# Latent attention two heads at a time: value products in 64-column groups, and the sums of the weights on GpSimd

## What is computed

```python
def dense_attention(q, k, v, scale):
    ...
        s = jnp.einsum('bqhgd,bkhd->bhgqk', qb, k).astype(jnp.float32) * scale
        p = jax.nn.softmax(s, axis=-1).astype(v.dtype)
        return jnp.einsum('bhgqk,bkhv->bqhgv', p, v)

def prefix_attention(q, k, v, q_c, k_c, v_c, scale, need_ctx):
    o = dense_attention(q, jnp.concatenate([k, k_c], axis=1), jnp.concatenate([v, v_c], axis=1), scale)
    o_c = dense_attention(q_c, k_c, v_c, scale) if need_ctx else None
    return o, o_c

def mla_mixer(h, h_c, rows, need_ctx, w_in, g_qa, w_qb, g_kva, w_kvb):
    ...
        q = (rms_norm(q_lat, g_qa) @ w_qb).reshape(bsz, n, A_HEADS, A_NOPE + A_ROPE)
        kv = (rms_norm(kv_lat, g_kva) @ w_kvb).reshape(bsz, n, A_HEADS, A_NOPE + A_V)
    ...
    o, o_c = prefix_attention(q, k, v, q_c, k_c, v_c, (A_NOPE + A_ROPE) ** -0.5, need_ctx)
    return gated(o, gate), (gated(o_c, gate_c) if need_ctx else None)
```

## Time and profile before

| | us |
|---|---|
| median of 3 runs | 1667.3 (1667.1 to 1669.59) |
| span of the profiled execution | 1666.1 |
| PE busy | 1582.5 (95%) |
| DVE busy | 1006.0 (60%) |
| POOL busy | 915.0 (55%) |
| ACT busy | 696.4 (42%) |
| latent attention, from the first scores to the last values | 859.3 to 1121.8 |

### The profile page before, as it was taken

How to read it: one execution, slowest core, us unless ns; L and a number is a source line. 1 busy time by engine, 2 the same in 40 slices (tenths; PEclk the granted TensorE clock), 3 DMA queues, 4 the chain that set the end, 5 groups by cost and what they waited for, 6 DMA issues and landing times.

```text
span 1666.1 us, 28604 instructions
## 1 busy us (share of the span) xinstructions
PE 1582.5 (95%) x11752; PEld 1282.3 (77%) x11752; DVE 1006.0 (60%) x1308; ACT 696.4 (42%) x1210; POOL 915.0 (55%) x722
## 2 busy tenths in 40 slices
PE   6999888999999999999989999999989999999887
PEld 5677787678888888878877777768877888888775
DVE  5699785746565540052465756664766665656566
ACT  4653775333222220042336565661154344444562
POOL 5354787838999999964550321346524444444152
PEclk9999999999999999999999999999899999999998
DMA  5221104422322243341120000003321101111211
GB/s 194 76 90 62 54 4 156 152 102 76 101 101 87 89 159 119 116 150 51 51 76 1 26 1 26 1 4 148 127 90 51 48 29 51 51 51 51 102 51 51
DMA packets 18881, 126.15 MB, mean 76 GB/s; under 512 B 2096, under 2 KB 2352, under 8 KB 4304
## 3 DMA queue, kind: packets, MB, share of 16 engines
q1 hardware_dynamic: 18624, 124.02, 21.2%
q10 hardware_dynamic: 144, 0.52, 0.1%
HBM read 122.43 MB, written 2.10 MB: 75 GB/s over the span
## 4 chain that ended last, share of the span: by engine, by line
PE 54%; issue 19%; POOL 12%; DVE 9%; ACT 4%; DMA 1%; POOLq 0%; ACTq 0%; SPq 0%; DVEq 0%
POOL w_hi L672 8%; PE banks L1324 5%; PE banks L1303 4%; POOL w_lo L663 4%; PE banks L1481 4%; PE banks L1484 4%; PE banks L1482 4%; PE banks L1186 3%; PE banks L1191 3%; PE banks L1187 3%; PE banks L1536 2%; PE banks L781 2%; PE banks L782 2%; PE banks L783 2%; PE banks L1516 2%
## 5 line engine op out<-in xcount | busy, mean ns | idle before, releaser
L672 POOL TENSOR_TENSOR w_hi<-raw,der 128x512 fp32r<-128x512 f32 x296 | 333.8, 1138 | 419.8 <-PE banks L1484 186.9
L663 POOL TENSOR_TENSOR w_lo<-raw,w_hi 128x512 fp32r<-128x512 f32 x336 | 479.6, 1440 | 61.9 <-ACT w_hi L1624 61.6
L781 PE MATMUL banks<-h_hi,w_hi 128*128 128x512 f32 x464 | 184.2, 397 | 0.3 <-DVEq L2308 0.3
L782 PE MATMUL banks<-h_lo,w_hi 128*128 128x512 f32 x464 | 180.7, 389 | 0.0
L783 PE MATMUL banks<-h_hi,w_lo 128*128 128x512 f32 x464 | 180.6, 389 | 0.0
L1481 PE MATMUL banks<-h_hi,w_hi 128*128 128x512 f32 (+1 forms) x384 | 146.3, 381 | 0.1
L1482 PE MATMUL banks<-h_lo,w_hi 128*128 128x512 f32 (+1 forms) x384 | 131.0, 356 | 0.0
L2145 ACT ACTIVATE dP<-banks,der 128x768 f32<-128x768 f32 x64 | 57.8, 902 | 160.2 <-DVE der L2981 160.2
L725 POOL TENSOR_TENSOR Of<-Of,Ls 128x768 f32<-128x768 f32 x8 | 14.7, 1834 | 186.6 <-DVE Ls L2783 186.6
L1484 PE MATMUL banks<-h_hi,w_lo 128*128 128x512 f32 (+1 forms) x384 | 116.1, 356 | 0.0
L781 PEld LDWEIGHTS banks<-h_hi,w_hi 128*128 128x128 f32 x464 | 87.1, 188 | 25.9 <-issue 7.5
(11 more groups left out here) (514 smaller groups left out, 3856.9 us busy)
## 6 DMA issues: line engine op xcount, KB each, us to landing
raw<-in_stream SPq DMA_DIRECT2D x84, 1024.0 KB, 4.9
ada_raw<-in_ada_w SPq DMA_DIRECT2D x18, 1024.0 KB, 7.1
raw<-in_ada_w SPq DMA_DIRECT2D x4, 1024.0 KB, 4.8
xT<-in_x_t SPq DMA_DIRECT2D x2, 1024.0 KB, 6.6
xT<-in_x_t SPq DMA_DIRECT2D x1, 2048.0 KB, 7.9
ada_end<-in_ada_w SPq DMA_DIRECT2D x2, 1024.0 KB, 5.9
out_t<-z SPq DMA_DIRECT2D x8, 256.0 KB, 2.1
ctxT<-in_ctx_t SPq DMA_DIRECT2D x1, 1024.0 KB, 6.9
```

The costliest lines, as they stand in the source:

```text
L663: return pool.tensor_tensor(lo[:, h, part(i), :], raw_tiles(half)[:, part(i), :], hi[:, h, part(i), :], ALU.subtract)
L672: pool.tensor_tensor(hi[:, h, part(i), :], raw_tiles(half)[:, part(i), :], one, ALU.mult).then_inc(hi_done, 1)
L781: pe.matmul(banks[b][:, :], hi, tile(rhs_hi, k), start=(at_k == 0), stop=False)
L782: pe.matmul(banks[b][:, :], hi, tile(rhs_lo, k), start=False, stop=False)
```

## The change

- PE computes the value products of both heads of a pair in one step: two fp32 products with 64 columns of weights each, one into the upper and one into the lower 64 partitions of bank 2. The steps of the two heads alternate (s = 0 to 13, head e = s % 2), the values follow in the odd s.
- The value tile has no ones and is one tile for the pair. The sums of the weights are made apart: POOL adds the exponentials of the pair's six key tiles (`add_part`, five additions of 128x1024 to Sx and one of 128x512 to Sc), and PE multiplies the sum with 64 columns of ones (`sums_x`, `sums_c`) in the next pair's steps 2 and 8, into bank 3. In the last pair DVE does these additions (`last_part`).
- ACT copies the result once for a pair (512 columns and 256) and no sums; DVE inverts straight out of PSUM. `finish` is cut in a part of 512 columns and one of 256.
- POOL's splits are cut in pieces between the additions.
- Queries have four buffers, exponentials three of 2x512, Of and Ls one. The order of every engine is written anew, the start of the stage too: `tops` of heads 0 and 1 go between the last input projections.

The core of the difference (buffer addresses, the sums behind the stage and the waits for counts that follow from the pairs are left out):

```diff
-        def values(h, j):
+        def values(p, j):
...
             if j < 6:
-                mm = pe.matmul(pairs[1][:, 0, :], v[:, j, :], Pf[:, i % 4, :], start=(j == 0), stop=(j == 5), skip_group_check=True)
+                for e in range(2):
+                    mm = pe.matmul(banks[2][HEAD[e], :], v[:, j, HEAD[e]], weighed[:, e, :], start=(j == 0), stop=(j == 5), skip_group_check=True)
...
+        def sums_x(p):
+
+            pe.wait_ge(*added(p, 5))
+            if p:
+                pe.wait_ge(sums_inverse, 3 * p)
+            for e in range(2):
+                mm = pe.matmul(banks[sum_bank(p, 0)][HEAD[e], :], ones[:, HEAD[e]], Sx[:, e, :], start=True, stop=True, skip_group_check=True)
+            mm.then_inc(sums_full.sem, 1)
...
+        scores(0)
+        for k in range(2):
+            query(2, k)
+        row(1)
+
+        TOP_SLOTS = [1, 2, 3, 4, 5, 7, 8, 9, 10, 11]
+        for p in range(N_PAIRS):
+            more = p < LAST_PAIR
+            for s in range(N_STEP):
+                if s == 6 and more:
+                    row(2 * p + 2)
+                if s == 12 and more:
+                    row(2 * p + 3)
+                if N_STEP * p + s + 1 < N_STEP * N_PAIRS:
+                    scores(N_STEP * p + s + 1)
+                if s == 0 and p == 0:
+                    key(1)
+                if more and s in (1, 2):
+                    query(2 * p + 3, s - 1)
+                if more and s in TOP_SLOTS:
+                    t = TOP_SLOTS.index(s)
+                    tops(2 * p + 2 + t // 5, t % 5)
+                if s == 2 and p:
+                    sums_x(p - 1)
+                if s == 8 and p:
+                    sums_c(p - 1)
+                if more and s in (5, 6):
+                    value_tokens(p + 1, range(3 * (s - 5), 3 * (s - 5) + 3))
+                if s in (8, 9) and p + 2 < N_PAIRS:
+                    query(2 * p + 4, s - 8)
+                if s == 12 and p + 2 < N_PAIRS:
+                    key(p + 2)
+                if s % 2:
+                    values(p, s // 2)
...
+            for s in range(N_STEP):
+                weigh_keys(N_STEP * p + s)
+                if s == 0 and p:
+                    output_c(p - 1)
...
+                if s == 0 and more:
+                    key_hi(p + 1, 1)
...
+                if s == 12:
+                    output_x(p)
+                if s == 13 and further:
+                    query_hi(2 * p + 4)
+                    key_hi(p + 2, 0)
...
+            top(a, 0)
+            top(a, 1)
+            rope_query(b)
+            rope_query_sum(b)
+            top(a, 2)
+            if p:
+                inverse(p - 1, 0)
+            top(a, 3)
+            top(a, 4)
```

More of the change, by code:

```diff
@@ L720, in _ @@
         assert (before - first) % 2 == 0
[L722 to L734 removed]
+        split(BLK1, 0, BLK1 // 2)
@@ new lines, in finish, with split_steps @@
+        def finish(p, c):
+            cols = slice(T, TA) if c else slice(0, T)
+            pool.wait_ge(sums_inverse, 3 * p + 2 + c)
+            pool.wait_ge(oc_copied if c else ox_copied, p + 1)
+            pool.tensor_tensor(Of[:, cols], Of[:, cols], Ls[:, cols], ALU.mult).then_inc(pair_divided, 1)
+            pool.wait_ge(pair_divided, 2 * p + 1 + c)
+            pool.tensor_tensor(gate_s[:, p, cols], gate_s[:, p, cols], Of[:, cols], ALU.mult).then_inc(pair_out, 1)
+        def split_steps(n, first, count):
+            split(n, half_of(n), n // 2, steps=range(first, first + count))
@@ new lines, in _ @@
+        n = BLK1 + 1
+        for p in range(LAST_PAIR):
+            first_half = p % 2 == 0
+            split_steps(n, 0 if first_half else 6, 2)
+            if not first_half:
+                n += 1
+            for j in (1, 2, 3):
+                add_part(p, j)
+                if first_half and j < 3:
+                    split_steps(n, j + 1, 1)
+            if p:
+                finish(p - 1, 0)
+            add_part(p, 4)
+            if p:
+                finish(p - 1, 1)
+            add_part(p, 5)
+            if first_half:
+                split_steps(n, 4, 1)
+            add_part(p, 6)
+            if first_half:
+                split_steps(n, 5, 1 if p < LAST_PAIR - 1 else 3)
@@ L735, in _ @@
+        n += 1
+        finish(LAST_PAIR - 1, 0)
+        finish(LAST_PAIR - 1, 1)
+        split_steps(n, 0, 2 * PARTS)
+        n += 1
+        finish(LAST_PAIR, 0)
+        finish(LAST_PAIR, 1)
         if n % 2:
@@ L1351, in _ @@
         key(0)
-        mla_in(10, range(0, 4))
-        value_tokens(0, range(6))
-        mla_in(10, range(4, KT))
-        for k in range(2):
-            query(1, k)
+        for k in range(KT):
+            mla_in(10, [k])
+            if k == 1:
+                for q in range(2):
+                    query(1, q)
+            if k == 4:
+                value_tokens(0, range(6))
+            if k >= 4:
+                tops(0, k - 4)
         for k in range(KT):
             mla_in(11, [k])
-            if k in (0, 2, 3, 5, 6):
-                tops(0, (0, 2, 3, 5, 6).index(k))
@@ L1361, in _ @@
-        row(0)
-        scores(0, 0)
-        for h in range(A_HEADS):
-            nxt, after = h + 1, h + 2
-            for j in range(N_S):
-                if j == 5 and nxt < A_HEADS:
-                    row(nxt)
-                if j < 6:
-                    scores(h, j + 1)
-                elif nxt < A_HEADS:
-                    scores(nxt, 0)
-                if j < 5 and nxt < A_HEADS:
-                    tops(nxt, j)
-                if after < A_HEADS:
-                    if j in (0, 2):
-                        query(after, j // 2)
-                    if h % 2 == 0 and j == 4:
-                        key(after // 2)
-                    if h % 2 and j in (4, 5):
-                        value_tokens(after // 2, range(3 * (j - 4), 3 * (j - 4) + 3))
-                values(h, j)
@@ L1382, in _ @@
-        pe.wait_ge(exp_done, N_S * A_HEADS)
+            if k == 0:
+                tops(0, 4)
+            if k == 2:
+                row(0)
+            if k >= 3:
+                tops(1, k - 3)
+        scores(0)
[31 more added lines that the diff above has]
+                    values(p, s // 2)
```

389 lines of the change are left out of this document (208 added, 181 removed).

## The result

| | before | after |
|---|---|---|
| median, us | 1667.3 | 1724.0 (1721.4 to 1725.2) |
| ratio after / before | | 1.0337, interval 1.0324 to 1.0350 |
| span of the profiled execution | 1666.1 | 1719.6 |
| end of the first `key_lo` of the loop | 880.2 | 871.5 |
| end of the seventh | 1081.0 | 1115.6 |

What follows compares the result with a forecast made beforehand. PE was taken to bound the kernel, busy 232.8 of 234.2 us in mid-stage. Three stretches, -5.8 (start), +26.2 (pairs 0 to 5) and +13.4 (end), sum to +33.8, taken as +33 on 1667.3: 1700 us, range 1676 to 1716.

Steps and rivals of the forecast that it cites:

- pair 0: First pair of the loop, without sums and inverses: 29.5 us of work, waits 1.7 + 1.6 + 2.3, half clock 1.5; put at 37.
- What PE is spared: PE's value products: 1.18 us a step side by side, saving 1.85 a pair; PE's work falls from 33.3 to 31.4.
- Rival (B): Values steps: the two column groups don't overlap, 1.72 us a step, total 1715; chance 0.10 together with rival (D).
- The four waits: New PE waits in each pair from the new order: 7.0 us summed, less 0.4, so 6.6; a pair takes 38.0.
- (1): First head, tops 1 to tops 4: DVE needs 6.8 us, PE 5.2, so PE waits 1.6; POOL adds 0.35 a pair.
- (2): Second head, tops 2 to tops 4: DVE needs 5.2 us, PE 4.0, so PE waits 1.2.
- (3): The second row, behind the query's sum and a reduction: 0.1 us of waiting without POOL, 1.45 more with POOL's addition.
- (4): The pair's boundary, from second row to next query: ACT and DVE need 7.3 us, PE 5.0, so PE waits 2.3.
- rival (D): Idle of 2.3 us at each pair's boundary lowers the clock, up to 1.7 a drop; chance 0.10 together with Rival (B).
- The start: To the end of the loop's first `key_lo`, at 874.5: 43.3 us, 5.8 less than before, with two casts at 3.08.
- The end: From the seventh `key_lo` to the last pair's product: 70 us instead of 56.8, put at 13.4 more.
- no meeting of POOL and DVE: Same waits in a pair, but POOL's additions miss DVE's sums: 36.6 us a pair; as rival 1690 to 1675, chance 0.12.

Runs made afterwards that it cites:

- Run 14: Run 12 with one POOL instruction moved: the low half of a split stands behind the third addition, not the second; 1667.4 us, ratio 1.000 to the kernel before.
- Run 1: The change with spare PE products of 512 columns put into its waits, adding nothing to the result: 1711.5 us, ratio 1.026 to the kernel before.
- run 8: Run 5 with start order and last OT_HI copy moved, value products one after the other over all 128 columns: 1707.4 us, against 1676.5 side by side.
- run 10: Run 5 with start order and last OT_HI copy moved, then DVE's query sum and last inverse, ACT's copies and POOL's context finish reordered: 1702.9 us, ratio 1.020.
- run 12: Run 11 with ACT's two late query copies moved and POOL's splits at the stage's end begun earlier: 1682.2 us, ratio 1.009 to the kernel before.
- run 5: The change with DVE's inverses and query sum moved, and the key ahead of the second row at the pair's boundary: 1679.8 us, ratio 1.007.
- run 11: Run 10 with the stage's end reordered, ACT's query copies moved (high half behind step 5's exponential) and fifth tops issued later: 1672.7 us, ratio 1.003.

## Why the prediction was wrong

By its own three stretches and the time behind them, in the profiled execution (1719.6, forecast 1699.1):

| | forecast | measured |
|---|---|---|
| first `key_lo` ends | 874.5 | 871.5, -3.0 |
| pair 0 | 37 | 37.3, +0.3 |
| pairs 1 to 5 | 190 | 206.8, +16.8 |
| to the last pair's product | 70 | 78.0, +8.0 |
| behind it | 528.3 | 526.0, -2.3 |

The rest, 0.7, is that 33.8 was rounded to 33. Two of the rows hold scatter. The count begins where the input projection of the last gates begins, and that was at 830.16 in this execution, 1.0 us before the 831.15 of the forecast; the 2.3 behind the last pair's product lie in the scatter of the part behind the output projection.

**What PE is spared: right.** A values step costs 1.20: from 1000.85 (the tops ahead of it start their last product of 0.12 at 1000.73) to 1002.28, less 0.23 for the first product of the next scores, where 1.18 was forecast from the 32-column pair of the earlier trace rows. Rival (B), no overlap, fell.

For the rest of the pair the waits have to be counted by the distance of starts, since the brackets count from the modelled end of a product. Take the first wait: the last product ahead of it starts at 1002.51, the second behind it at 1004.23. Between them lie two products of 0.23, so 1.26 us were lost, and not 0.99. Part of that is that a product which starts behind a wait, or behind another tiling, takes 0.34 and not 0.23 (1003.89 to 1004.23, and 1001.94 to 1002.28). Counted so, the five waits cost 1.26, 1.44, 1.41, 1.35 and 2.03, together 7.5, where the brackets say 6.36. PE's own work in a pair is then 38.7 - 7.5 = 31.2, as forecast (31.4). The pair of before holds 0.35 of waiting by the same count, so its work was 33.1, and 1.9 are saved, where 1.85 was forecast. Run 14's two waits cost 0.76 and 0.88 by this count, so it saves 33.1 - (33.2 - 1.6) = 1.5.

**The four waits: right in place, 0.9 short in size.** By the distance of starts: (1) 1.26 + 1.44 = 2.7, forecast 1.6 and 0.35 for POOL; (2) 1.4, forecast 1.2; (3) 1.35, forecast 1.55; (4) 2.0, forecast 2.3. Together 7.5, where the prediction summed to 7.0 and took 0.4 off, because a late reduction in (1) would partly hide in the next; (1) came out longer even without that. That an addition holds DVE's sum was right (2.04 where 2.1 was worked out); in (1) it does so in every pair and not in every other, and makes it 1.65 instead of 0.68. This misses the time by 0.7 us a pair, 3.5 us in pairs 1 to 5.

**The clock: the step that failed.** The prediction took one fall, at the start, into the sum, and as rival (D) wrote "A drop costs up to 1.7; included above 1700". The mechanism was named, and nothing was put into the sum for any later pair. The price was low too: no row shows 1.7, and the fall in the earlier trace rows cost 2.6 by the prediction's own count. The earlier trace rows had the warning: PE came back at half its clock from 3.97 us of idle, and the new order has idle of 1 to 2 us, four times in each of seven pairs, where before PE had 0.6% of idle in the whole loop. Measured: 13.3 us in pairs 1 to 5; in the rest of the stage (pair 6 from 1127.5 and the last pair from 1168.5) some 5 more, half of 6.8 and 3.4 us. A stretch of 6.8 us made a pair 2.7 to 3.2 us longer, two of 3.4 us together 2.8. Run 1 shows it as a cause, by 13.1 us in the same pairs. With hindsight the right term is one fall in most pairs; by an estimate of 2 to 3 us in six pairs from these figures the forecast would have stood at 1712 to 1718, and its range, moved as far, would have held the result. What sets off a fall in one pair and not in the next stays open.

**The start: 3 us better, 1 of them scatter.** The other 2 are the casts. The two casts of KLO took 1.11 us in all, not 3.08 as in the earlier trace rows. The trace of before has the reason, a POOL instruction that I had not laid beside them, and the change runs POOL's splits earlier:

```profile
861.53 3.55 POOL L663 TENSOR_TENSOR w_lo<-raw,w_hi 128x512 fp32r<-128x512 f32 x2
```

In the change:

```profile
867.45 1.11 DVE L2912 CAST KLO<-KLO 32x768 fp32r<-32x768 f32 x2
...
871.66 0.76 PE L1253 MATMUL banks<-lat_hi,w_hi 128*128 128x512 f32 x1 [6.64 <-DVE KLO L2857]
```

**The end: 8 us worse.** 4.4 of them lie in pair 6 (3.4 by the clock, an estimate: half of 6.8). In the last pair PE waited 2.78 us for an exponential behind a copy that waited for POOL's `finish`, where I had allowed 2.5 for all waits, and 0.78 again; then for low halves and the last chain:

```profile
1167.83 0.84 ACT L2120 ACTIVATE OT_HI<-gate_s 128x768 fp32r<-128x768 f32 x1 [3.38 <-POOL gate_s L769]
...
1169.21 1.98 PE L1390 MATMUL banks<-Pf,V 128*64 128x512 f32 x4 [2.78 <-ACT Pf L2104]
...
1181.67 0.50 PE L1253 MATMUL banks<-OT_HI,w_hi 128*128 128x512 f32 x1 [0.72 <-DVE OT_LO L2893]
...
1193.60 0.50 PE L1253 MATMUL banks<-OT_HI,w_hi 128*128 128x512 f32 x1 [1.59 <-DVE OT_LO L2893]
```

The two heads' products share their rows and differ in columns, and run side by side: the four records of a step span 1.08 us (the row at 1000.93), where the two of one head's full-width product span 1.02. A step costs 1.20, and run 8 pays 0.57 more. The rule of the Trainium skill that was weighed (TensorE: Matmul & The Clock Gate, Part 3: a weight load overlaps running products only where the row group differs) would have given 1.72 if taken at its word; here too the measurement decides against it.

**Three sums of the prediction don't come out as they are put.** With no meeting of POOL and DVE its own terms give 38.0 - 1.45 - 0.35 = 36.2 a pair and not 36.6; the last stretch, 70 less 56.8, is 13.2 and not 13.4; and the terms of pair 0 add to 36.6, put at 37. Each moves the time by less than 3 us, and none changes the outcome. Of the 3.0 us under the forecast at the start 1.0, and the 2.3 behind the stage, are scatter and not foresight; without them the miss in the profiled execution would be 23.8 and not 20.5, as it is 24 by the medians.

## What to carry to other kernels

Where a change gives a saturated TensorE idle of a microsecond or more, count the clock with it in every round of the loop: here the waits cost 7.5 us a pair, and the half clock, which came once or twice in four pairs of five, up to 4.7 more. A saving on the bounding engine is only as large as the slack of the chains that feed it; of 1.9 us a pair the best order tried kept 0.2 (33.23 against 33.46), and nothing of it shows in the time of the whole. And when an instruction is moved on one engine, look up who waits for it on every other: two of the orders tried here (runs 10 and 12) lost 26 and 10 us to a wait that the move itself had made.

## What the runs showed of the hardware

- The same waits did not always bring the half clock: of five pairs with the same waits one had none and another had it for some 10 us. In runs 5, 14 and 11, whose waits in pairs 1 to 5 are at most 0.5, 0.6 and 0.9 us, none of these pairs had it; in run 10, with one wait of 1.95 us in each, every one had. What decides between the pairs of the change is not shown.
- Two casts of 32x768, with one SBUF input, took 3.08 us beside POOL's low halves (which took 3.55 for two themselves, and 2.5 elsewhere) and 1.11 with POOL idle. The slow case stands in one trace alone, that of before.
- DVE's 128x768 subtraction took 0.96 us alone and 2.85 beside a 128x1024 addition, more than that addition's 2.36: it ended 0.8 us behind it.
- The reciprocal read from PSUM costs what it did from SBUF, 1.75 us.
